# Pooling matrices sent in bf16 and fp32 parts and widened by GpSimd, and a last weight row sent in two column parts

## What is computed

```python
n = rms_norm(x, norm1_w); q, k, v, u = split(n @ w_in)
a = sliding_window_attention(rope(qk_norm(q)), rope(qk_norm(k)), v, sinks)   # window 128
for g, w in enumerate((2, 4, 8, 16)):                    # causal means of the last w tokens
    pooled[:, g] = (csum - lagged(csum, w)) / minimum(pos + 1, w) - u[:, g]
p = einsum('bsgc,gcd->bsgd', pooled, pool_w) * pool_scale
h = x + concat(a, p) @ w_out
logits = rms_norm(h, norm2_w) @ w_router + b_router      # top 4 of 32, softmax of the 4
y = h + sum over the chosen e of gate_e * (swiglu(n2 @ w_gu[e] + b_gu[e]) @ w_down[e] + b_down[e])
```

## Time and profile before

| | us |
|---|---|
| median of 3 runs (988.5 to 988.91) | 988.81 |
| the profiled execution | 988.7 |
| its span in the trace | 986.9 |
| TensorE busy | 946.6 |
| DVE busy | 202.9 |
| ACT busy | 127.7 |
| GpSimd busy | 14.0 |

### The profile page before, as it was taken

One profiled execution on the slowest core, in us unless ns is written; L12 is line 12 of the kernel. 1 busy time (PEld: TensorE's weight loads), 2 busy tenths in 40 slices (PEclk: granted clock), 3 DMA queues, 4 the chain that ended last, 5 costly groups with the idle time before them and its releaser, 6 DMA issues.

```text
span 986.9 us, 11112 instructions
## 1 busy us (share of the span) xinstructions
PE 946.6 (96%) x4508; PEld 382.4 (39%) x4508; DVE 202.9 (21%) x610; ACT 127.7 (13%) x346; POOL 14.0 (1%) x9
## 2 busy tenths in 40 slices
PE   9999999999999899898989989889989999999997
PEld 5545433333333334333333333333333333333432
DVE  4645121212111121210112121011212112111121
ACT  2433111011110111010011101001101110011101
POOL 0031000000000000000000000000000000000000
PEclk9999999999999999999999999999999999999999
DMA  9999999999999999999999999999999999999996
GB/s 374 426 423 398 412 429 434 432 430 428 432 431 429 436 430 430 434 432 429 434 433 426 437 432 428 437 430 429 436 429 431 432 429 430 431 433 430 422 422 272
DMA packets 23869, 418.27 MB, mean 424 GB/s; under 512 B 2912, under 2 KB 3296, under 8 KB 8224
## 3 DMA queue, kind: packets, MB, share of 16 engines
q1 hardware_dynamic: 23408, 417.20, 99.2%
q10 hardware_dynamic: 432, 0.66, 0.2%
HBM read 416.80 MB, written 1.05 MB: 423 GB/s over the span
## 4 chain that ended last, share of the span: by engine, by line
PE 63%; DMA 36%; DVE 1%; issue 0%; ACT 0%; SPq 0%; DVEq 0%
DMA ring<-w_gu_dram 33%; PE ps L1237 29%; PE ps L1342 14%; PE ps L1205 4%; PE ps L1189 4%; DMA ring<-w_down_dram 3%; PE ps L1066 3%; PE ps L997 2%; PE ps L1004 1%; PE ps L1293 1%; PE ps L1301 1%; PE ps L1013 0%; PE ps L1039 0%; PE ps L1058 0%; PE ps L1046 0%
## 5 line engine op out<-in xcount | busy, mean ns | idle before, releaser
L1237 PE MATMUL ps<-ring,passing 128*64 128x512 f32 x1008 | 229.1, 604 | 14.8 <-DMA ring<-w_gu_dram 14.8
L1237 PE MATMUL ps<-ring,PR 128*64 128x512 f32 x976 | 224.5, 608 | 16.4 <-DMA ring<-w_gu_dram 16.2
L1342 PE MATMUL ps<-ring,PT 128*64 128x512 f32 x984 | 218.3, 595 | 0.5 <-DMA ring<-w_down_dram 0.5
L952 DVE TENSOR_SCALAR xw<-ps 128x256 f32<-128x256 f32 x64 | 27.2, 425 | 650.0 <-PE ps L1237 650.0
L1237 PEld LDWEIGHTS ps<-ring,passing 128*64 128x64 f32 x1008 | 76.8, 139 | 158.3 <-issue 143.8
L1237 PEld LDWEIGHTS ps<-ring,PR 128*64 128x64 f32 x976 | 74.9, 140 | 157.0 <-issue 145.4
L1342 PEld LDWEIGHTS ps<-ring,PT 128*64 128x64 f32 x984 | 68.1, 137 | 129.6 <-issue 127.5
L652 ACT ACTIVATE xw<-xw 128x256 f32<-128x256 f32 x64 | 26.6, 416 | 484.5 <-DVE xw L952 484.5
L1205 PE MATMUL ps<-PT 64*128 64x512 f32 x248 | 69.7, 640 | 0.0
L1189 PEld LDWEIGHTS ps<-qk,X 128*128 128x128 f32 x512 | 59.6, 191 | 18.8 <-issue 18.8
L1189 PE MATMUL ps<-qk,X 128*128 128x128 f32 x512 | 65.7, 281 | 0.0
(11 more groups left out here) (198 smaller groups left out, 374.6 us busy)
## 6 DMA issues: line engine op xcount, KB each, us to landing
ring<-w_gu_dram SPq DMA_DIRECT2D x48, 4096.0 KB, 28.2
ring<-w_down_dram SPq DMA_DIRECT2D x25, 4096.0 KB, 29.7
ring<-w_gu_dram SPq DMA_DIRECT2D x14, 2048.0 KB, 14.2
ring<-w_gu_dram SPq DMA_DIRECT2D x6, 3072.0 KB, 23.2
ring<-w_down_dram SPq DMA_DIRECT2D x5, 2048.0 KB, 23.1
ring<-w_gu_dram SPq DMA_DIRECT2D x9, 1024.0 KB, 9.6
ring<-w_down_dram SPq DMA_DIRECT2D x8, 1024.0 KB, 25.9
ring<-w_down_dram SPq DMA_DIRECT2D x2, 3584.0 KB, 27.6
```

The costliest lines, as they stand in the source:

```text
L952: nc.vector.tensor_scalar(gb[:, b, :], gu[:, b, 0, :], LIMIT, None, ALU.min).then_inc(g_ready, 1)
L1237: last = mm(ps[64 * j:64 * j + 64, GU + b, :], lhs, halves[j][:, 512 * b:512 * b + 512], start=start, stop=stop)
L1342: last = mm(ps[64 * j:64 * j + 64, bank, :], at[:, k, 64 * (c - GU_PIECES):64 * (c - GU_PIECES) + 64], rows[:, 512 * j:512 * j + 512], sta ...
```

## The change

The pooling matrices have two kinds of columns. The first 16 columns of a group divide by the number of tokens so far and stay fp32 (`edge`). All others hold fractions with a power of two below, which bf16 holds exactly, and the columns of the second 128 tokens repeat those of the first, but for 16. So 144 bf16 and 16 fp32 columns a group are sent, 1408 bytes a partition in place of 4352 (180,224 bytes in place of 557,056), to a place behind `poolw`. GpSimd writes `band` from them with four copies, and TensorE waits for `unpacked` at the first use and for `ld_poolw` at the third. The last row block of the last expert comes as two DMAs, each with 256 of the 512 columns of both halves, as runs of 1 KB where there were runs of 4 KB. The product with it, ACT's copy and the final addition are cut into the same columns.

```diff
@@ -45,6 +45,8 @@
+EDGE = max(POOLS)
+PACKED = NG * (P + EDGE) // 2 + NG * EDGE
@@ -64,7 +66,8 @@
 END_CUTS = {(2, 2): ((4, 6), (6, 8)), (3, 0): ((0, 2), (2, 4)), (3, 2): ((4, 6), (6, 7), (7, 8)),
-            (2, 4): ((0, 2), (2, 4), (4, 6), (6, 7), (7, 8)), (3, 4): ((0, 2), (2, 4), (4, 6), (6, 7), (7, 8))}
+            (2, 4): ((0, 2), (2, 4), (4, 6), (6, 7), (7, 8)), (3, 4): ((0, 2), (2, 4), (4, 6), (6, 7))}
+LAST_COLUMNS = ((0, 256), (256, 512))
 X_CUTS, W_CUTS = ((0, 1), (1, 2), (2, 4), (4, 8)), ((0, 1), (1, 2), (2, 3), (3, 4), (4, 6), (6, 8))
@@ -111,7 +114,9 @@
-    return c, mask.astype(np.float32), freq.astype(np.float32), passed.astype(np.float32), order, bands.reshape(P, NG * (REACH + P))
+    exact = np.concatenate([bands[:, :, EDGE:REACH], bands[:, :, REACH:REACH + EDGE]], 2).astype(mybir.dt.np(BF16))
+    packed = np.concatenate([exact.reshape(P, -1).view(np.float32), bands[:, :, 0:EDGE].reshape(P, -1)], 1)
+    return c, mask.astype(np.float32), freq.astype(np.float32), passed.astype(np.float32), order, packed
@@ -201,6 +206,9 @@
+        packed = front[:, KC * INW + NG * (REACH + 2 * P):KC * INW + NG * (REACH + 2 * P) + PACKED]
+        exact = packed[:, 0:NG * (P + EDGE) // 2].bitcast(BF16).rearrange("p (g s) -> p g s", g=NG)
+        edge = packed[:, NG * (P + EDGE) // 2:PACKED].rearrange("p (g s) -> p g s", g=NG)
@@ -384,8 +395,8 @@
             sp.dma_start(wu, w_u.rearrange("p (k n) -> p k n", k=KC)).then_inc(ld_u, 16)
-            sp.dma_start(band, bands.rearrange("p (g s) -> p g s", g=NG)).then_inc(ld_bands, 16)
-            sp.dma_start(poolw, w_pool.rearrange("p (g n) -> p g n", g=NG)).then_inc(ld_bands, 16)
+            sp.dma_start(packed, bands).then_inc(ld_bands, 16)
+            sp.dma_start(poolw, w_pool.rearrange("p (g n) -> p g n", g=NG)).then_inc(ld_poolw, 16)
             mix = w_mix.rearrange("p (k n) -> p k n", k=KC)
@@ -493,6 +504,11 @@
                         load(slot, row, src, k * wide - base, stop * wide - base).then_inc(landed_end[u, c, k], 16)
+                    if (u, c) == (TURN - 1, GU_PIECES):
+                        ends = ring[:, slot * PIECE + PAIR - DM:slot * PIECE + PAIR].rearrange("p (j n) -> p j n", j=2)
+                        rows = src[:, row, PAIR - DM:PAIR].rearrange("p (j n) -> p j n", j=2)
+                        for q, (a, b) in enumerate(LAST_COLUMNS):
+                            sp.dma_start(ends[:, :, a:b], rows[:, :, a:b]).then_inc(landed_cols[q], 16)
                 else:
@@ -512,6 +528,10 @@
         def _(pool):
+            pool.wait_ge(ld_bands, 16)
+            for dst, src in ((band[:, :, EDGE:REACH], exact[:, :, 0:P]), (band[:, :, REACH + EDGE:REACH + P], exact[:, :, 0:P - EDGE]),
+                             (band[:, :, REACH:REACH + EDGE], exact[:, :, P:P + EDGE]), (band[:, :, 0:EDGE], edge)):
+                nc.gpsimd.tensor_copy(dst, src).then_inc(unpacked, 1)
             f = bias[0:3 * NE, :, :].rearrange("p t n -> p (t n)")
@@ -675,7 +695,9 @@
             down_out(NE - 2, GU_PIECES)
-            down_out(NE - 1, 0, GU + 1, ye_last)
+            act.wait_ge(pieces_used, NE * PIECES)
+            for done, (a, b) in zip((y_first, y_sb), LAST_COLUMNS):
+                nc.scalar.copy(ye_last[:, a:b], ps[:, GU + 1, a:b]).then_inc(done, 1)
@@ -1087,7 +1109,7 @@
-            pe.wait_ge(ld_bands, 32)
+            pe.wait_ge(unpacked, 4)
             pe.wait_ge(uv_out, 3)
@@ -1097,6 +1119,7 @@
             attend(0)
+            pe.wait_ge(ld_poolw, 16)
             for g in range(NG):
@@ -1338,10 +1361,14 @@
                             wait_landed(c)
-                        for j in range(2):
-                            last = mm(ps[64 * j:64 * j + 64, bank, :], at[:, k, 64 * (c - GU_PIECES):64 * (c - GU_PIECES) + 64],
-                                      rows[:, 512 * j:512 * j + 512],
-                                      start=c == GU_PIECES and k == 0, stop=c == PIECES - 1 and k == 3)
+                        in_columns = step == "last" and c == PIECES - 1 and k == 3
+                        for q, (a, b) in enumerate(LAST_COLUMNS if in_columns else ((0, 512),)):
+                            if in_columns:
+                                pe.wait_ge(landed_cols[q], 16)
+                            for j in range(2):
+                                last = mm(ps[64 * j:64 * j + 64, bank, a:b], at[:, k, 64 * (c - GU_PIECES):64 * (c - GU_PIECES) + 64],
+                                          rows[:, 512 * j + a:512 * j + b],
+                                          start=c == GU_PIECES and k == 0, stop=c == PIECES - 1 and k >= (2 if step == "last" else 3), skip_group_check=in_columns)
                         if k == 3:
@@ -1400,10 +1427,14 @@
             pe.wait_ge(gt_sb, NE)
-            pe.wait_ge(y_sb, NE)
             for t in range(T):
-                for last in to_tokens(t, GT_last, ye_last):
-                    last.then_inc(acc_final, 1)
+                for q, (a, b) in enumerate(LAST_COLUMNS):
+                    pe.wait_ge(*((y_first, 1), (y_sb, NE))[q])
+                    for j in range(2):
+                        last = mm(ps[:, ACC[t] + j, a:b], GT_last[64 * j:64 * j + 64, t, :], ye_last[64 * j:64 * j + 64, a:b],
+                                  start=False, stop=True, skip_group_check=True)
+                        if b == 512:
+                            last.then_inc(acc_final, 1)
...
                 for u in range(TURN):
```

More of the change, by code:

```diff
@@ L305, in layer_kernel @@
         landed_end = {(u, c, k): sem(f"landed_end{u}_{c}_{k}") for (u, c), parts in END_CUTS.items() for k, _ in parts}
+        landed_cols = [sem(f"landed_cols{q}") for q in range(len(LAST_COLUMNS))]
         ld_aside = [sem(f"ld_aside{k}") for k in range(2)]
@@ L311, in layer_kernel @@
         split = sem("split")
+        ld_poolw, unpacked = sem("ld_poolw"), sem("unpacked")
         cleared = sem("cleared")
@@ L341, in layer_kernel @@
         gt_psum, gt_sb, y_sb = sem("gt_psum"), sem("gt_sb"), sem("y_sb")
+        y_first = sem("y_first")
         more_done = sem("more_done")
```

## The result

The changed kernel took **990.34 us** (median of 16 runs, 989.26 to 993.52) beside 989.1 for the kernel before in the same runs: a ratio of 1.0018, with an interval from 1.0010 to 1.0026. I had forecast 987.8 and a range up to 989.4. By the medians the change costs 1.2 us, by the ratio 1.8 (1.0 to 2.6), where I had it save 1.0.

The account below looks back on a forecast made before the run. TensorE bounds the first third, then the weight stream at 430 GB/s sets the end. Savings of 0.88 and 0.20 us less 0.05 make 1.03 us, so 987.8 us from a median of 988.81; range 986.8 to 989.4.

Parts of the forecast that it names:

- The pooling matrices' bytes: Front loads on SP's queue: 376,832 bytes fewer at 430 GB/s, 0.88 us less stream, all of it on the path.
- 2.4 us of reserve: SP's queue at about 112.5 us: at least 2.4 us of work before every issue, enough to bear 1.5 us.
- the stand-in: End-of-kernel store with nothing before it, 3.1 us, used as the landing time of an unloaded 512 KB read.
- the case at 0.08: Rival on SP's queue: reserve under 1.5 us somewhere, queue runs empty, saving lost to TensorE's pace, 988.7 us; chance 0.08.
- The sign in the windows: DMA windows around the tightest place: share 1.03 and 1.02 at 401 and 381 GB/s meant slower packets, not an empty queue.
- my sign of being wrong: DMA windows between 40 and 130 us: a share clearly under 1 would show the prediction wrong.
- GpSimd's copies: Four copies of 1088 columns at the front: 1.3 us, upper bound 2.5, over by 25 us.
- The 20 us of cover: Between the copies' end at 24.3 us and TensorE's first use at 44.7: the wait for `unpacked` costs nothing.
- nothing in the sum, whether DVE is held or not: Norms at 23 to 25 us: GpSimd may hold DVE 1.3 us, TensorE 0.65 us late, borne by the reserve.
- The column parts: Last row block in two parts at the kernel's end: small packets 0.18 us, ACT's copy starts 0.20 us sooner.
- The final additions: Kernel's end: sixteen half-width instructions in place of eight, 0.05 us more.
- uneven finish: Rival at 974 to 978 us: engines over 1.5 us behind others even out, 986.3 us; chance 0.10.

Follow-up runs that it names:

- e5: Kernel before, with one chunk of the second token half's u projection computed twice, TensorE about 0.9 us later from 39 us on: 990.17 us, ratio 1.0011.
- e12: Changed kernel with 24 waits on a long reached semaphore added on TensorE ahead of the last expert's first row block: 989.91 us, ratio 1.0005.
- e14: Kernel before, with one of eight chunks of the second token half's u projection left out, TensorE 0.9 us earlier: 989.06 us, ratio 0.9999.
- e7: Kernel before, with the last down row block loaded in two 256-column transfers, but multiplied, copied and added whole: 989.27 us, ratio 1.0000.
- e2: Kernel before, with only the last weight row in two column parts and its copies and final addition cut likewise: 989.75 us, ratio 1.0008.
- e3: Changed kernel, with GpSimd's four copies held until DVE's second norms of q and k are done: 989.72 us, ratio 1.0008 to before.
- e15: Changed kernel, with GpSimd's copies held until DVE's norms are done and 24 idle waits added on TensorE: 988.84 us, ratio 0.9994 to before.
- e13: Kernel before, with the same 376,832 bytes left out of one weight pair of the third last turn of experts: 988.31 us, ratio 0.9989.

## Why the prediction was wrong, step by step

**The bytes' price was right, their place was not.** The failing step is "The pooling matrices' bytes": "All of it lies on the path if the queue never runs empty: the stream has 2.4 us of reserve at its tightest place". I had made the 2.4 from the landing time of 5.5 us less 3.1 us for a store with nothing before it. The 5.5 is the median of two loads, not the shortest; the first of them landed in 4.8, the second in 6.2. The same view of after, and word for word of e5 and e12, whose stream runs dry at this place, gives for these two loads

```profile
ring<-w_gu_dram SPq DMA_DIRECT2D x2, 512.0 KB, 4.8
```

So 4.8 us is what such loads take, on the median of the two, with next to nothing in front of them, and the reserve was at most 5.5 - 4.8 = 0.7 us, too little for 0.88. For the first load alone, which was 4.8 in the kernel before, after has

```profile
ring<-w_gu_dram SPq DMA_DIRECT2D x1, 512.0 KB, 4.3
```

and e12 4.2, which leaves 0.5 to 0.6. The table by TensorE's start puts it at some 0.55 us in a run with an early TensorE, and none in the profiled one. I had named the stand-in as the weak point and still put the case at 0.08.

**The sign in the windows was read the wrong way.** I took 401 and 381 GB/s at a share of 1.03 and 1.02 for slower packets. From 114 to 118 and 118 to 122 us e14, with TensorE early, has 411 and 437 GB/s, where before has 391 and 393, so in part it was a queue with too few transfers in it. And e12, whose stream is the farthest behind, shows shares of 1.01 and 1.00 at 360 GB/s. The two rows of each:

```profile
114.00:118.00 4.00, 4.00 (x22) 1.38 (x20) 0.00 (x0) 0.41 (x1) 0.00 (x0) 1.00 1.02 411
118.00:122.00 4.00, 4.00 (x20) 1.29 (x18) 0.00 (x0) 0.17 (x1) 0.00 (x0) 1.00 1.05 437
```

```profile
114.00:118.00 4.00, 4.00 (x20) 1.29 (x18) 0.00 (x0) 0.00 (x0) 0.00 (x0) 1.00 1.01 360
118.00:122.00 4.00, 4.00 (x22) 1.34 (x20) 0.00 (x0) 0.59 (x1) 0.00 (x0) 1.00 1.00 360
```

So my sign of being wrong, a share clearly under 1, would not have shown even this; the rate does.

**GpSimd's copies: duration right, cover wrong.** Forecast 1.3 us; measured 1.48, from 23.61 to 25.09. The 20 us of cover in front of the pooling products hold. What failed is "nothing in the sum, whether DVE is held or not". I had the hold at 1.3 us and it was 0.70. I had DVE's last step before the transposes end at 29.1, and it did (29.03), but by luck: 0.5 us of that lateness was there before GpSimd began, a lateness of the front part that I had in no step. I had TensorE 0.65 us late, and against an ordinary run, with the transposes at 28.0 to 28.5, it is 0.6 to 1.2. The reserve that should have borne it was not there. The exclusive lock that the Trainium skill states (SBUF — State Buffer, section on the two separate sides) agrees with the trace for two DVE steps: one ended at 24.25 and one at 24.74, where GpSimd's first two casts ended at 24.22 and 24.73. It does not for the next one. That step reads two SBUF operands and ran in 0.17 us from 24.78, while the third cast is recorded from 24.67 to 24.91 (GpSimd's times in a profile are rough).

**The column parts: the first step right, the sum wrong.** The weight load of the first part was to start 7.07 us behind the first row block's products; it did (978.03 - 970.96). The second part's was 0.05 sooner than forecast. The small packets cost nothing that shows (e7's ratio is 1.0000, and the second part's weight load had no wait for data). But from the first part's load to ACT's copy it is 1.51 us (979.54 - 978.03), where the whole block took 1.22 and I had 1.30. These 0.21 us eat the 0.20 of gain. e2, with the same tail, has 1.50. The final additions took 1.89 us, where I had 1.93.

**The place that was missing.** 0.9 us outside the span, in no step and no rival. e12 shows that it is no price of the change's work. This alone would have carried the time from my 987.8 to 988.7, inside my range. A further 0.3 us is the base: the kernel before came out at 989.1 in these runs, where I had started from 988.81.

The terms that I forecast as -0.88, -0.20 and +0.05 are thus near 0, 0 and 0. After has 0.9 more outside the span and, by the medians of its times and its spans, 0.3 to 0.65 more in it. The held DVE covers that in the whole change: without it the span falls by 1.0 to 1.15 us (e3, e15). The middle half of after's spans lies within 2.0 us and that of before's within 0.5. In part that may follow from the table, since without a reserve each lateness of TensorE is passed on.

It is not all. The time at which 10 MB were left to load was, beside the kernel before's, 0.8 us later in e3 and 1.8 in e12. But the last expert's first row block, at 970.90 there, came 2.6 and 3.1 us later:

```profile
973.54 1.94 PE L1370 MATMUL ps<-ring,xw 128*64 128x512 f32 x8 [1.24 <-DMA ring<-w_down_dram]
```

```profile
974.00 1.94 PE L1371 MATMUL ps<-ring,xw 128*64 128x512 f32 x8 [1.34 <-DMA ring<-w_down_dram]
```

The first row is of e3, the second of e12. So these two profiled runs, the slowest of their kernels, lost 1.8 and 1.3 us more in how the last bytes landed, where the other fifteen traces differ by under 0.7. What decides that is open, and no experiment here moved it; it is the "uneven finish" that I had listed as a chance of gain.

A lateness of TensorE that no edit made shows in e7's windows at 88 to 92 us, where the granted clock (the third last column) fell to the lower of its two levels, 1.2 GHz, and expert 0's down started 0.9 us later than in e13 (111.45 against 110.53, with the transposes of both at 28.0):

```profile
86.00:88.00 2.00, 2.00 (x19) 2.00 (x18) 1.50 (x10) 2.00 (x7) 0.00 (x0) 0.93 1.11 358
88.00:90.00 2.00, 2.00 (x14) 1.94 (x14) 1.25 (x9) 0.80 (x4) 0.00 (x0) 0.50 1.02 358
90.00:92.00 2.00, 2.00 (x15) 2.00 (x15) 1.06 (x5) 0.00 (x0) 0.00 (x0) 0.72 0.97 397
```

It stood at 1.00 there in 13 of the 17 traces. It fell in e3, e5, e7 and e15, two with the front part and two without, so it is not tied to the change. In e7 TensorE was busy without a gap at 86 to 88 us, but so it was in e13, where the clock stayed at 1.00, and in e5 it was busy for 1.73 of these 2 us.

What stays open: why all eight kernels with the front part move only 333 to 357 GB/s from 3 to 7 us, where the others move 376 to 405, and whether DVE's first norm is 0.5 us later for that (in bytes little is lost: by 80 us the eight have moved 0.06 MB less than the kernel before on the mean, the others 0.03 less); what spreads the last landings; and what is late behind the span.

## What to carry to other kernels

Ask of saved bytes not only what they cost but what the next stretch downstream waits for: bytes saved ahead of a stretch in which each load waits for a slot were worth next to nothing here, and behind it their full price (0 and 0.85 us for the same 0.38 MB). The reserve of a queue is its landing time less that of the same kind of load in a queue known to be dry, never less a store's, and of single loads, not of a median; cheaper still, make the consumer 1 us late on purpose and see whether the end moves. One profiled run is one draw: a term under 1 us should be read from several, since the start of TensorE's transposes alone differed by 0.9 us between runs of the same front.

## What the runs showed that I had not expected

- The time outside the span is not a constant: 1.8 us in twelve kernels, 2.35 and 2.4 in two, 2.7 to 3.0 in three, and 24 idle waits brought it from 2.7 back to 1.8.
- An early delay of 0.9 us on TensorE made the whole kernel 1.1 us longer although TensorE waits 31 us for data later on.
- Two 512 KB loads took 4.3 and 5.2 us to land in a nearly empty queue, against 3.1 us for a store of the same size.
- The mean DMA share stayed at 1.00 and 1.01 in a stretch where the rate was 360 GB/s and the queue ran dry.
- A step of DVE on 128x10 elements went from 0.17 to 0.58 us beside a GpSimd cast.
